# Transposes of a pooling/attention trunk taken from TensorE to the DMA queue, with several pieces of work put in another order

## The reference

```
def pool_mixer(h, w_in, w_grp, scale, w_out):
    u, z = split(h @ w_in, 2)                # 2048 channels each; 4 groups of 512 for u
    t = trailing mean of u over w tokens - u # w = 2, 4, 8, 16 by group
    y = (t @ w_grp per group) * scale * silu(z)
    return y @ w_out

def gla_mixer(h, w_in, w_gate2, b_gate, head_norm, w_out):
    q, k, v, z, glr = split(h @ w_in)        # 4 heads: dk 256, dv 512; glr has rank 16
    log_a = log_sigmoid(glr @ w_gate2 + b_gate) / 16
    # chunk by chunk, with cum = inclusive cumsum of log_a in the chunk:
    qe, ke = q * exp(cum), k * exp(-cum)
    o = tril(qe @ ke.T) @ v + qe @ S
    kd = k * exp(cum[-1] - cum)              # decayed keys
    S = exp(cum[-1]) * S + kd.T @ v
    return (rmsnorm(o) per head * head_norm * silu(z)) @ w_out
```

## Time and profile before

| | us |
|---|---|
| median of the runs | 2021.51 |
| lowest of the runs | 2020.16 |
| the profiled execution | 2020.69 |
| its span, first to last instruction, core 5 (the slowest) | 2019.1 |
| the fastest core's span (core 0) | 2007.8 |
| TensorE busy in the span | 1946.3 |
| VectorE busy | 1537.6 |
| ScalarE busy | 1140.2 |
| GpSimd busy | 248.8 |

### The profile page before, as it was taken

One profiled execution on the slowest core, in us unless ns is written; L12 is line 12 of the kernel. 1 busy time (PEld: TensorE's weight loads), 2 busy tenths in 40 slices (PEclk: granted clock), 3 DMA queues, 4 the chain that ended last, 5 costly groups with the idle time before them and its releaser, 6 DMA issues.

```text
span 2019.1 us, 55182 instructions; the slowest of 8 cores (2007.8 to 2019.1 us)
## 1 busy us (share of the span) xinstructions
PE 1946.3 (96%) x20040; PEld 1412.0 (70%) x20040; DVE 1537.6 (76%) x2848; ACT 1140.2 (56%) x2475; POOL 248.8 (12%) x395
## 2 busy tenths in 40 slices
PE   4999999999999999999989999999999999999997
PEld 2677777767767767767767777776777677676775
DVE  3868777887767777777777688788777777777788
ACT  3433323467666666667764332334766666666787
POOL 1310000011111111111211100000211111111110
PEclk8999999999999999999999999999999999999999
DMA  9522305050032041040040403040400400400011
GB/s 278 124 36 51 67 8 84 1 85 2 2 53 45 2 63 24 2 75 2 2 74 1 75 12 74 1 84 1 85 2 12 85 2 2 85 2 2 33 65 74
DMA packets 16318, 89.96 MB, mean 45 GB/s; under 512 B 2562, under 2 KB 2818, under 8 KB 7604
## 3 DMA queue, kind: packets, MB, share of 16 engines
q0 software_dynamic: 9136, 59.45, 17.3%
q1 hardware_dynamic: 6772, 26.72, 4.0%
q10 hardware_dynamic: 144, 0.26, 0.0%
HBM read 137.47 MB, written 8.39 MB: 72 GB/s over the span
## 4 chain that ended last, share of the span: by engine, by line
PE 77%; ACT 8%; DVE 7%; issue 5%; DMA 2%; DVEq 0%; POOL 0%; ACTq 0%; SPq 0%; POOLq 0%
PE ps L462 21%; PE ps L533 12%; PE ps L716 9%; PE ps L762 8%; PE ps L748 8%; PE ps L912 7%; DVE arena L873 3%; DVE arena L852 3%; PE ps L314 3%; PE ps L862 2%; PE ps L830 2%; ACT hnT L391 1%; PE ps L388 1%; PE ps L826 1%; DMA W<-wpack 1%
## 5 line engine op out<-in xcount | busy, mean ns | idle before, releaser
L462 PE MATMUL ps<-hnT,W 128*128 128x256 bf16 (+1 forms) x4096 | 465.2, 274 | 2.1 <-DVE hnT L337 1.4
L462 PEld LDWEIGHTS ps<-hnT,W 128*128 128x128 bf16 x4096 | 400.4, 98 | 65.4 <-issue 2.7
L737 POOL TENSOR_SCALAR arena<-arena 128x128 bf16<-128x128 bf16 (+1 forms) x256 | 149.7, 585 | 1034.7 <-DVE arena L852 873.4
L912 PE MATMUL ps<-W,arena 128*128 128x512 bf16 (+1 forms) x1056 | 263.3, 379 | 9.7 <-DVE arena L852 7.3
L762 PEld LDWEIGHTS ps<-hnT,W 128*128 128x128 bf16 x4224 | 242.8, 98 | 31.0 <-issue 1.7
L920 DVE SCALAR_TENSOR_TENSOR h<-ps,arena,h 128x512 f32<-128x512 f32 (+1 forms) x264 | 198.0, 750 | 86.1 <-ACT arena L898 63.5
L748 PE MATMUL ps<-W,hnT 128*128 128x512 bf16 (+1 forms) x1088 | 258.1, 380 | 0.0
L716 PE MATMUL ps<-hnT,W 128*128 128x128 bf16 (+1 forms) x4288 | 255.7, 217 | 0.0
L762 PE MATMUL ps<-hnT,W 128*128 128x128 bf16 (+1 forms) x4224 | 253.4, 218 | 0.0
L533 PE MATMUL ps<-W,arena 128*128 128x512 bf16 (+1 forms) x1088 | 248.8, 381 | 3.4 <-POOL W L1078 3.4
L880 ACT ACTIVATE arena<-arena 128x1024 bf16<-128x1024 f32 x128 | 135.3, 1057 | 198.2 <-DVE arena L873 191.8
(11 more groups left out here) (90 smaller groups left out, 2508.3 us busy)
## 6 DMA issues: line engine op xcount, KB each, us to landing
W<-wpack POOLq DMA_DIRECT2D x53, 1024.0 KB, 16.4
h<-x SPq DMA_DIRECT2D x8, 1024.0 KB, 17.6
out<-h SPq DMA_DIRECT2D x15, 512.0 KB, 3.0
h<-wpack SPq DMA_DIRECT2D x4, 1024.0 KB, 27.1
W<-wpack POOLq DMA_DIRECT2D x7, 512.0 KB, 13.1
W<-wpack SPq DMA_DIRECT2D x3, 1024.0 KB, 14.1
gbc<-pool_norm SPq DMA_DIRECT2D x2, 512.0 KB
gbc<-gla_norm SPq DMA_DIRECT2D x2, 512.0 KB
```

Source lines behind the costliest of these rows:

```text
L462: ins = e.matmul(dst[:, f, 0:n], lhsT=Wm[:, 2 * q + f, kc, :], rhs=hnT[:, kc, c0:c0 + n], start=(kc == 0), stop=(kc == 7))
L737: P.op("pool", lambda e, dc=dc: e.tensor_scalar(out=kdT[par][:, dc, 0:n], in0=ke[par][:, dc, 0:n], scalar1=Eq[par][:, dc, n - 1:n], scalar ...
L912: ins = e.matmul(pout[0:n, :], lhsT=yT[par][:, ec, 0:n], rhs=Wo[:, ec, half * 512:(half + 1) * 512], start=(ec == 0), stop=(ec == 3))
```

## The change

Two kinds of transposes leave TensorE. Normalised tiles 1 to 16 of layers 1, 2 and 3 are transposed by one DMA each, issued from SyncE right behind `scale`, straight from `hnb` to `hnT`; `step` then only advances and, where asked, scales the next tile. The decayed keys of chunks 1 to 15 in every head of both GLA layers are transposed by one DMA each, from `kdT` to `kd`; `K2` has nothing to copy for them. Chunk 0, tile 0 and the whole first layer keep TensorE's transposes.

Work is put in another order as well. At the start the input comes first in SyncE's queue, three tiles are transposed ahead of the folds, the z weights are staged by halves, and the first three blocks run their projections before the first output projection. In a GLA layer `K` and the tile step stand earlier in a step, q and k of chunk 1 are computed inside the step of chunk 0 (ahead of the output projection of the head before), and the reciprocal roots for the next layer are computed behind `Q3` and `K` of that step. `pscale` and `hnorm` become one vector `vec`, loaded once. Output stores go to GpSimd's queue but for the last two tiles, and the last two chunks are closed in another order and with other PSUM banks.

```
+            if i > 0 and not self.from_x:
+                c0 = tile_col0(i)
+                P.dma("sp", s_hnt, [(lambda q: q.dma_start(out=hnT[:, :, c0:c0 + 128], in_=hnb[:, :], transpose=True), [b_hnb], [hnTb[i]])])
 
         def step(self, pbi, ahead=True):
...
             self.t += 1
+            if i > 0 and not self.from_x:
+                if ahead:
+                    self.scale(i + 1)
+                return
...
             def stageK(ci):
...
+                if ci > 0:
+                    P.dma("sp", s_kdt, [(lambda q: q.dma_start(out=kd[par].rearrange("p (f m) -> p f m", f=2),
+                                                               in_=kdT[par].rearrange("p f m -> p (f m)"), transpose=True),
+                                         [bQk[par]], [bK[par]])])
+                    return
...
             def stageK2(ci):
-                if ci == last:
+                if ci > 0:
                     return
...
         def run(norm, before, nxt, late=None):
...
+            if late is not None:
+                G = groups[0]
+                step = lambda a=True: norm.step(ring(), a)
+                G["A"](0, 0)
+                G["A"](0, 1, None, step)
...
+                G["A"](2, 0)
+                G["A"](2, 1)
+                step()
+                out_of(0)
...
-                G["A"](bi, 0, before if k == 0 else None)
-                slot()
+                if k == 0:
+                    G["A"](bi, 0, lambda: (slot(), before()))
+                else:
+                    G["A"](bi, 0)
+                    slot()
...
-                call("Q", k)
+                if k > 0 and steps[k - 1][1] > 0:
+                    call("Q", k)
...
                 call("Q3", k)
+                if ci > 0:
+                    call("K", k)
+                if nxt is not None and hd == 3 and ci == 12:
+                    rstd_of(0, 11)
                 call("V", k)
...
-                elif stepper is not None:
-                    stepper.step(3, False)
-                if ci > 0:
-                    call("K", k)
...
-                if prev:
-                    done_e(k - 1)
                 if ci == 0:
+                    call("Q", k + 1)
                     call("K", k)
+                if closing:
+                    call("E", k - 1, sums=1, part=1)
+                elif prev:
+                    done_e(k - 1, pbf=4 if ci == 0 else 0)
...
-                P.dma("sp", s_vec, [(lambda q, li=li: q.dma_start(out=pscale[:], in_=vecp[:, 8 * li:8 * li + 16]), [], [b_vec])])
```

More of the change, by code:

```diff
@@ L914, in mout @@
                         return ins
-                    P.op("pe", mout, [bYt[par], Wb[s][3]], PB(6 + half))
-                    if half == 0 and roots:
-                        stageF(ci)
+                    if part & 1:
+                        P.op("pe", mout, [bYt[par], Wb[s][3]], PB(pbo + half))
+                        if half == 0 and sums:
+                            stageF(ci, pbf, sums)
+                if not part & 2:
+                    return
                 for half in range(2):
-                    pout = pS[half]
+                    pout = bank(pbo + half)
                     P.op("dve", lambda e, half=half, pout=pout: e.scalar_tensor_tensor(
@@ L982, in run @@
                 bare = prev and fuse_final and steps[k - 1][1] == 0
+                closing = fuse_final and not more
                 stepper = None
@@ L1001, in run @@
                 call("Q2", k)
-                if more:
+                if more and prev:
                     call("G", k + 1)
@@ L1041, in run @@
                 call("K2", k)
-                call("Z", k, begun=not more)
+                call("Z", k, begun=0 if more else 2 if closing else 1)
+                if closing:
+                    call("F", k - 1, part=2)
                 if more:
@@ L1045, in run @@
                 call("D", k)
-                if prev:
+                if prev and not closing:
                     maybe_final(k - 1, 0)
@@ L1099, in build @@
     load_x(2, "sp")
-    load_x(3, "sp")
     stage(5, hfl[:, 13 * D:15 * D], w0[:, 12288:14336], [hb[13], hb[14]])
     stage(6, hfl[:, 15 * D:17 * D], w0[:, 14336:16384], [hb[15], hb[16]])
+    load_x(3, "sp")
+    P.op("act", lambda e: e.activation(out=lnv[:, 0:1], in_=epsc[:, 0:1], func=AF.Square), [b_one], [b_stat[0]])
+    n0.prep(1)
+    n0.scale(1)
+    n0.prep(0)
+    n0.t = 1
+    n0.step(6, False)
+    n0.scale(2)
+    n0.step(7, False)
+    n0.scale(0)
+    n0.t = 0
+    n0.step(6, False)
@@ L1104, in build @@
+    n0.t = 3
     cast("pool", W0[:, 8192:10240], st1[:, 4096:6144], [Wb[1][2]], [Wb[0][2]])
-    cast("dve", v4(W0[:, 0:4096])[:, :, 0:512], v4(st1[:, 0:4096])[:, :, 0:512], [Wb[1][0]], [b_half[0]])
-    n0.prep(0)
-    n0.scale(0)
-    for dc in range(2):
+    cast_u(0, "dve")
+    for dc in range(4):
         fold(0, dc, dc, "act" if dc % 2 else "dve", [b_half[0]])
-    n0.step(6, False)
-    n0.prep(1)
-    for dc in range(2, 4):
-        fold(0, dc, dc, "act" if dc % 2 else "dve", [b_half[0]])
@@ L1123, in build @@
+    n0.prep(3)
+    n0.scale(3)
+    cast_z(1, "pool")
     load_x(4, "sp")
```

151 lines of the change are left out of this document (98 added, 53 removed).

## The result

The changed kernel is slower. It took 2106.64 and 2102.74 us, the kernel before 2018.74 to 2021.51 on the same chip: a ratio of 1.0419, with a 95% interval of 1.0388 to 1.0449. Forecast were 1960 us and a range of 1942 to 2030. The profiled run took 2106.64 us, 85.9 more than the 2020.7 of before.

A forecast was written before the change was run, and what follows sets the result against it. The prediction took PE (TensorE) as the bound, busy 1946.3 of 2019.1 us. Savings of 71.5 us and 10 us of DMA cost made 2020.7 - 71.5 + 10 = 1959.2, so 1960 us, range 1942 to 2030.

The forecast's parts named there:

- the one on packets: Key DMAs beside unit loads: one or two packets an engine, landing by 5.4 us, within 5.5 of slack; cost 0.
- rival 1: GLA layers: unit loads delay the key DMAs; 1977 us, or 2046 at 12.5 us to landing; chance 0.17.
- +10 us: Tile DMAs in three loads: about three tiles each, 1 us late apiece, rounded up; between 0 and 9 x 3.5.
- the transposes that leave TensorE: 120 key transposes (13.2 us) and 48 tiles (21.1 us) no longer take PE time: 34.3 us saved.
- the gate input's waits: First head of each GLA layer: PE's waits for PSUM bank 3 before the gate input go, 13.3 us saved.
- Heads: Head borders: the output projection's waits for VectorE go because q and k stand in front, 7.5 us saved.
- the roots and the second gate: PE's waits in the last head's chunk 12 and at layer 3's second gate go: 1.8 and 1.2 us saved.
- Layer 2: Start of layer 2: PE's idle 5.5 us, with the late pscale load, mostly goes, 4.5 us saved.
- Start: Kernel start: earlier first projection and no wait for the output projection's weight cast, 7.4 us saved (0 to 12).
- End: Kernel end: the changed closing order saves part of 9.1 us idle, 1.5 us (0 to 3).
- rival 4: The rearrangements move waits instead of removing them, PE loses only 34.3 us: 1986 to 1996 us; chance 0.08.
- Rivals 2 and 3: 2: a tile's DMA outlasts a step, 1992 to 2048 us, 0.06; 3: keys late in every step, about 2128, 0.14.

The follow-up runs named there:

- experiment 1: The changed kernel with all transposes back on TensorE, so only the new order of instructions and loads: 2012.8 to 2014.3 us, ratio 0.985 to the kernel before.
- experiment 7: The changed kernel with GLA-layer unit loads issued in pieces behind each step's transposes, layer-2 tiles up to 8 on TensorE: 1969.7 to 1973.1 us, ratio 0.965.
- experiment 5: The changed kernel with plain copies in place of the transposing DMAs, same buffers and bytes: 2068.8 to 2072.0 us, ratio 1.013 to the kernel before.
- experiment 6: The changed kernel with its unit loads cut into rows an eighth as long, same bytes: 2043.0 to 2064.3 us, ratio 1.007 to the kernel before.
- experiment 9: The changed kernel with all transposes on TensorE and the start (first loads, casts, folds, blocks) of the kernel before: 2037.7 to 2039.8 us, ratio 0.995.

## Why the prediction was wrong

**The step that failed** is the one on packets: "in one or two packets an engine, 3 us unhindered + 2 x 1.2 = 5.4 at most, in time; in 16, far more. I take the few large packets". It is one packet a row, 18 on an engine for the keys, where the prediction had one or two, and 68 for a tile, where it had five. The mechanism in front of that choice was right: a packet waits for one of the load, 0.6 to 1.2 us by the earlier trace rows, 0.65 to 0.80 measured. With 18 of them the prediction's own sum gives 2.3 + 18 x 0.65 to 0.80 = 14 to 17 us, far beyond the slack of 5.5; 15.7 to 19.1 were measured, and the rest is the late first packet, which the prediction didn't have. The argument for few packets, that 512 KB can't land in 3.0 us in small ones, does not hold: 256 KB did in 3.1 us in packets of 256 bytes, where no other queue was busy. An unhindered landing time says nothing about packets, and nothing about a busy queue.

So rival 1 is what happened, at five loads 10.6 to 13.3 us each, where its upper price was 14 for two steps. What no rival had is the tiles: for them **+10 us** was counted, and 70.3 came. Their bound, 12.5 us to landing, was taken from a DMA of nine packets on an engine; with 68 the DMA doesn't end until about when the load does (37.0 us at most), and everything behind it waits for that: a key DMA behind a late tile too, which landed after 21.0 us, where the prediction had it not held up. Put together, 2020.7 less 34.3, 13.3 and 7.8 (below), plus 131.2, makes 2096.5 us; of the 10 us left to 2106.6, the low clock behind a wait explains at least a part (2.3 us at the one shown), and no run takes them apart.

**Right:** the transposes that leave TensorE (34.3 us) and the gate input's waits (13.3). From experiment 1 to experiment 7 the distance from the first to the last state update shrinks from 1564.6 to 1522.8 us, and the span by 43.2; the two terms less the eight layer-2 tiles that experiment 7 has on TensorE (3.5 us) are 44.1. The gate inputs of two steps of layer 1's first head start 9.10 us apart in the changed kernel (489.70 and 498.80), before 10.15 (485.43 and the 495.58 of the earlier trace rows): 1.0 us less, as forecast.

**Too large:** the rearrangements, 24 us by the terms, 7.8 in the spans. Heads: "The 32 matmuls of q and k now stand in front" is so, but for the 7.5 us of waits that went, 6.0 came to the state update; with the roots and the second gate this leaves 4.5 us of 10.5. Layer 2: the wait of 3.57 us of the earlier trace rows is gone, a new one of 1.27 us (before the sums of squares) has come, and on core 0 of before the 3.57 us did not occur at all. Start: 2.0 of 7.4, above. End: the three waits of 0.68, 0.84 and 1.65 us that now stand there (3.2 us) are nearly as long as the two of 1.23 and 2.15 that they replace. This is rival 4 in small: each wait had a named cause, but the next cause stood right behind it, and I had looked at that only at layer 2.

**Rivals 2 and 3** are refuted: unhindered, keys land in 2.3 us and tiles in 3.1, far inside their slack of 5.5 and 9.0.

Unhindered, the plain copies of experiment 5 landed after 1.8 us (keys) and 2.9 us (tiles), the transposing ones after 2.3 and 3.1. That is near what the Trainium skill says in Advanced Engine Details and Errata (X-Bar Transpose (TRN2)), that transposing DMAs are as fast as others. The Trainium skill's figure in VectorE: DVE Perf Modes (The three transpose paths), by which a tile would have taken an estimated 10.5 us, is not what a single DMA of eight blocks takes here: 3.1 us. The advice of the same page of the Trainium skill (Rules for kernel authors) to transpose on TensorE where the result may lie in PSUM holds in this kernel where a unit loads, for a reason that neither section gives.

## What to carry to other kernels

Before a step is moved to a DMA, count its packets on each engine, and multiply by the time of one packet of whatever else runs on these engines then: that and a late start (some 3 us here), not its unhindered landing time, is what has to fit into the slack. If it doesn't fit, move the large transfer out of the way (in pieces, behind the landing of the small one) rather than the small one back. And when a wait is taken away, look up what the same engine waits for next: here 7.5 us of waits went at the head borders, and 6.0 of others came.

## What the runs showed of the hardware

- Two queues took turns by packet, though their packets differed in length by a factor of 27: 108 and 108 in 5 us, 0.75 MB against 0.03. It is not always one for one: with load packets of 1 KB it was 290 of the load to 229, and at the start of layer 2, between 1085 and 1105 us with tiles in the queue, it was 110 of the load beside 540, and the load itself slowed, to 46 GB/s in all. That this is why the tile took 37.0 us there is likely, but was not tried.
- A key DMA's first packet moved 3.8 to 4.8 us after its issue when a load ran, with load packets of 1 KB as with 7, and 1.1 us after it without a load. Why is open.
- The granted clock can stay at 0.81, between its two levels, for some 160 us with PE busy throughout, on some cores of a die and not on others: after the old start, and on two cores after a wait in the profile of experiment 6. It costs some 26 us a time. It came with the old start in all runs of experiment 9, though not in the profile that the prediction was made from, and with the new start on two cores in one of 13 runs.
